# A fused transformer block: the gated linear unit and four of ten feature-major pairs computed with seven block products in place of eight

## The reference

```python
y = jax.nn.gelu(y).astype(u.dtype)                 # end of the state-space mixer
a, g = jnp.split(y @ w_glu, 2, axis=-1)            # gated linear unit, 1024 -> 2048
x = x + a * jax.nn.sigmoid(g)
x = x + sqrelu_mlp(rmsnorm(x, norm_ffn[i]), mlp_w1[i], mlp_w2[i])   # (relu(h w1))^2 w2
gate = jax.nn.sigmoid(rmsnorm(x, norm_ple[i]) @ ple_gate_w[i])
x = x + (p[i] @ ple_w[i]) * gate
x = rmsnorm(x, norm_final)
...
h = rms_norm(x, norm_g_2)                          # second block
proj = h @ w_in_2                                  # to attention, mLSTM and convolution columns
```

## Time and profile before

| what | value |
|---|---|
| median of 3 runs | 3498.07 us (3496.97 to 3499.93) |
| the profiled execution: its own time, its span | 3496.82 us, 3495.1 us |
| mean granted clock of TensorE | 0.978 of full |
| busy: PE, DVE, POOL, ACT | 94%, 53%, 41%, 32% |
| GLU, first half of the tokens: first matmul to the MLP's | 341.86 to 521.50 us |
| FM starts, first half / second half | 1280.77 / 2599.40 us |
| second half of the tokens begins | 1664.59 us |

### The profile page before, as it was taken

The page is one execution under the profiler, slowest core; times in us unless marked ns, Lnnn a source line. Parts: engine busy times, 40 slices in busy tenths (PEclk is TensorE's granted clock), DMA queues, the critical chain, the costliest instruction groups (busy, mean ns, idle before and its releaser), DMA issues. The chain is left out here.

```text
span 3495.1 us, 43699 instructions
## 1 busy us (share of the span) xinstructions
PE 3298.3 (94%) x16369; PEld 2688.0 (77%) x16369; DVE 1841.0 (53%) x2234; ACT 1133.2 (32%) x1725; POOL 1443.9 (41%) x1008
## 2 busy tenths in 40 slices
PE   5877999999999999999999999999999999697799
PEld 5655877888888778888887888888778888376687
DVE  8785126454545766970125554545766961455421
ACT  4322124333333551112224333333542111565411
POOL 6810225566666412232325565656512241243522
PEclk8988999999999999999999999999999999899899
DMA  3344211111111213233311111111213231416543
GB/s 124 102 107 113 78 49 48 55 48 54 49 53 49 95 37 127 97 121 115 121 49 48 55 49 53 49 53 50 89 48 121 93 125 55 173 63 205 175 137 116
DMA packets 155796, 301.13 MB, mean 86 GB/s; under 512 B 16640, under 2 KB 91904, under 8 KB 154000
## 3 DMA queue, kind: packets, MB, share of 16 engines
q1 hardware_dynamic: 139504, 257.23, 23.7%
q10 hardware_dynamic: 16160, 42.08, 3.1%
HBM read 226.33 MB, written 72.94 MB: 86 GB/s over the span
## 5 line engine op out<-in xcount | busy, mean ns | idle before, releaser
L1739 PE MATMUL ps_job<-AHL,WH 128*128 128x512 f32 x4480 | 1384.4, 390 | 28.6 <-POOL WL L1298 27.0
L1298 POOL TENSOR_TENSOR WL<-WR,WH 128x1024 fp32r<-128x1024 f32 x216 | 522.7, 2420 | 1205.7 <-ACT WH L996 1204.0
L1739 PEld LDWEIGHTS ps_job<-AHL,WH 128*128 128x128 f32 x4480 | 842.5, 188 | 207.3 <-issue 19.1
L1739 PE MATMUL ps_job<-AHL,WL 128*128 128x512 f32 x2240 | 873.1, 390 | 0.0
L996 ACT CAST WH<-WR 128x1024 fp32r<-128x1024 f32 x216 | 226.9, 1051 | 1007.7 <-PE ps_job L1739 823.9
L1739 PEld LDWEIGHTS ps_job<-AHL,WL 128*128 128x128 f32 x2240 | 421.7, 188 | 88.2
L1494 DVE SCALAR_TENSOR_TENSOR ps_job<-ps_job,RB 128x1024 f32<-128x1024 f32 (+1 forms) x80 | 79.9, 1017 | 410.3 <-PE ps_job L1739 396.2
L1318 POOL TENSOR_TENSOR OPS_L<-VS,OPS_H 128x1024 fp32r<-128x1024 f32 (+2 forms) x96 | 193.6, 2030 | 55.9 <-ACT OPS_H L1122 51.3
L1411 DVE TENSOR_TENSOR VS<-ps_job,VS 128x1024 f32<-128x1024 f32 x16 | 19.6, 1225 | 363.1 <-PE ps_job L1739 363.1
L1836 PE MATMUL ps_job<-OPS_H,WH 128*128 128x512 f32 x512 | 199.4, 389 | 0.7 <-POOL WL L1298 0.7
L1836 PE MATMUL ps_job<-OPS_L,WH 128*128 128x512 f32 x512 | 199.2, 389 | 0.0
(11 more groups left out here) (428 smaller groups left out, 5684.6 us busy)
## 6 DMA issues: line engine op xcount, KB each, us to landing
WR<-in_wall SPq DMA_DIRECT2D x244, 512.0 KB, 3.5
fm_scratch<-VS ACTq DMA_DIRECT2D x32, 512.0 KB, 2.6
tm_scratch<-VS ACTq DMA_DIRECT2D x24, 512.0 KB, 2.7
s_U<-in_x_group SPq DMA_DIRECT2D x8, 1024.0 KB, 14.7
s_mt<-z_scratch SPq DMA_DIRECT2D x64, 128.0 KB, 4.8
prod_scratch<-s_Win SPq DMA_DIRECT2D x16, 512.0 KB, 2.6
X<-in_x_feat SPq DMA_DIRECT2D x2, 4096.0 KB, 14.5
m_oz<-tm_scratch SPq DMA_DIRECT2D x8, 1024.0 KB, 7.7
```

What stands on the lines that cost most here:

```text
L1298: pool.tensor_tensor(dst, raw, src.bitcast(F32), ALU.subtract).then_inc(raw_free, 1)
L1739: last = pe.matmul(out, l, r, start=(k == 0 and i == 0), stop=(k == k_tiles - 1 and i == 2))
```

## The change

Each pair of weight tiles of GLU but the first two (6 of 8) and the pairs 2 to 5 of FM (tiles 4 to 11, 4 of 10) are computed as one product of 2 by 2 blocks: two output tiles, two halves of the input features, two halves of the tokens. Seven block products of 4 x 3 = 12 matmuls of 128x512 do it, 84 a pair, where two tiles took 96.

The activation blocks need four differences, `T1` to `T4`. VectorE makes them in `YR` from the unsplit activations, once for GLU and once for FM, ScalarE casts them to `T_H` (8 casts), VectorE and GpSimd subtract for `T_L` (4 each). Each pair needs the sums S1, S2, S3, S4 of its weight blocks (GpSimd, `pair_weights`), their casts (ScalarE) and low parts (GpSimd); stored tiles are the blocks W11|W12 and, in place, S3|W22. ScalarE takes three intermediate results out of PSUM (`keep_first`, `keep_second`, `keep_fifth`), VectorE puts the seven together (`corner`, `third_sum`, `first_tile`, `second_tile`).

In FM the order is changed: `copy` tiles ahead of `conv` (`KINDS`, and `ORDER` for the weights and stores); the pairs are the `silu` and `copy` tiles. The taps of the long convolution start at tile 12. `convolve` makes its first tap with an operation of three operands in place of a tensor_scalar. The rows of `X` go out in three parts in place of two, and scratch for the norms is moved.

```diff
+ORDER = [*range(0, 8), *range(16, 20), *range(8, 16)]
+N_STD, FM_END = 2, 6
-KINDS = ["c_b"] * 2 + ["c_a"] * 2 + ["silu"] * 4 + ["conv"] * 8 + ["copy"] * 4
+KINDS = ["c_b"] * 2 + ["c_a"] * 2 + ["silu"] * 4 + ["copy"] * 4 + ["conv"] * 8
-TAPS_AT = {j: 3 for j in range(4, 8)} | {j: 2 for j in range(8, 16)} | {j: 3 for j in range(16, N_COPY)}
+TAPS_AT = {j: 2 for j in range(2 * FM_END, N_FM)} | {j: 3 for j in range(N_FM, N_COPY)}
...
@@ scalar, FM @@
+                for k in range(KD // 2):
+                    act.activation(YR[:, k], X[:, k], ACT.Copy, scale=gains[:, 3, k:k + 1]).then_inc(x_raw, 1)
                 act.preload_act_table_set("natural_log_exp_and_others")
                 last_norms()
...
+                act.wait_ge(job_done, job0 + (JOB_FM + 1))
+                whi(wf + 1, 0)
+                for c, k in ((2, 0), (4, KD // 2)):
+                    act.wait_ge(t_raw, 8 * tb + 4 + c)
+                    t_high(2 * tb + 1, range(k, k + KD // 2))
+                take(0)
+                act.wait_ge(job_done, job0 + (JOB_FM + 2))
+                whi(wf + 1, 1)
...
@@ gpsimd @@
+                def pair_weights(n, w, b, first, last_free=None):
...
+                    if not first:
+                        first_tile_low()
+                    pool.wait_ge(raw_loaded[0], 16 * w2 + 16)
+                    pool.wait_ge(raw_loaded[1], 16 * w2 + 16)
+                    pool.wait_ge(q6_done, n)
+                    pool.tensor_tensor(raw[:, 0], c[:, 0:HB], c[:, HB:], ALU.add).then_inc(wsum_done, 1)
+                    pool.wait_ge(wsum_done, 3 * n + 1)
+                    pool.tensor_tensor(c[:, 0:HB], a[:, 0:HB], c[:, 0:HB], ALU.subtract).then_inc(wsum_done, 1)
+                    pool.tensor_tensor(raw[:, 1], raw[:, 0], a[:, 0:HB], ALU.subtract).then_inc(wsum_done, 1)
+                    if first:
+                        first_tile_low()
...
+                    pool.wait_ge(q3_done, n)
...
+                    pool.tensor_tensor(raw[:, 2], a[:, HB:], raw[:, 1], ALU.subtract).then_inc(raw_free, 1)
...
+                    pool.wait_ge(wsh_done, 2 * n + 1)
+                    pool.tensor_tensor(sl[:, 0:2], raw[:, 0:2], sh[:, 0:2].bitcast(F32), ALU.subtract).then_inc(wsl_done, 1)
+                    pool.wait_ge(hi_done, w + 2)
+                    pool.tensor_tensor(WL[1][:], c[:], WH[1][:].bitcast(F32), ALU.subtract).then_inc(raw_free, 1)
+                    pool.wait_ge(wsh_done, 2 * n + 2)
+                    pool.tensor_tensor(sl[:, 2], raw[:, 2], sh[:, 2].bitcast(F32), ALU.subtract).then_inc(wsl_done, 1)
...
@@ vector, FM @@
+                dve.tensor_tensor(f11, f12, f11, ALU.subtract).then_inc(t_raw, 1)
...
+                for k in range(KD // 2):
+                    step = scaled_less(YR[:, k, half(1)], KD // 2 + k, 1, YR[:, k, half(1)])
+                step.then_inc(t_raw, 1)
+                for k in range(KD // 2):
+                    step = scaled_less(YR[:, KD // 2 + k, half(0)], KD // 2 + k, 1, YR[:, k, half(0)])
+                step.then_inc(t_raw, 1)
+                dve.wait_ge(t_raw, 4 * n + 3)
+                for k in range(KD // 2):
+                    step = scaled_less(YR[:, KD // 2 + k, half(1)], KD // 2 + k, 0, YR[:, KD // 2 + k, half(0)])
+                step.then_inc(t_raw, 1)
+                dve.wait_ge(t_raw, 4 * n + 4)
                 last_norms()
...
@@ tensor @@
+                def win_pair(n, b, slots, w, t_set, free, first):
...
+                    pe.wait_ge(wl0_done, n + 1)
+                    free(0)
+                    one(1, u, stop=False).then_inc(q1_done, 1)
+                    one(2, a).then_inc(q2_done, 1)
+                    pe.wait_ge(wsl_done, 2 * n + 1)
+                    free(1)
...
+                    one(5, v)
...
+                    pe.wait_ge(c1_kept, n + 1)
+                    one(6, u, start=False, stop=False).then_inc(q6_done, 1)
+                    pe.wait_ge(raw_free, w + 4)
+                    one(7, c).then_inc(q7_done, 1)
+                    pe.wait_ge(u2_kept, n + 1)
+                    pe.wait_ge(wsl_done, 2 * n + 2)
+                    one(3, u, start=False).then_inc(q3_done, 1)
+                    pe.wait_ge(u3_done, n + 1)
+                    one(4, c).then_inc(job_done, 2)
```

More of the change, by code:

```diff
@@ new lines, in _ @@
+                act.wait_ge(job_done, job0 + (JOB_FM + 3))
+                whi(wf + 2, 0)
+                store_rows(1)
+                act.wait_ge(st_x[0], 16 * tb + 16)
+                sums_high(n, FM)
+                store_rows(2)
+                last_sum_high(n, FM, TILE_FM + 2 * N_STD)
+                act.wait_ge(job_done, job0 + (JOB_FM + 4))
+                second_tile_high(n, wf + 2)
+                for i in range(N_STD, FM_END):
+                    n, last = N_WIN * tb + GLU_WIN + i - N_STD, i == FM_END - 1
+                    slots = [slot_of(2 * i + t) for t in range(2)]
+                    keep_first(n, FM, slots[0])
+                    act.wait_ge(q2_done, n + 1)
+                    whi(wf + i + 1, 0)
+                    if i > N_STD:
+                        finish_tile(2 * i - 2)
+                    keep_second(n, FM, slots[0])
+                    keep_fifth(n, FM, slots[1])
+                    if i > N_STD:
+                        finish_tile(2 * i - 1)
+                    if not last:
+                        sums_high(n + 1, FM)
+                        last_sum_high(n + 1, FM, TILE_FM + 2 * i + 2)
+                    act.wait_ge(job_done, job0 + (JOB_FM + 2 * i + 2))
+                    if last:
+                        whi(wf + i + 1, 1)
+                    else:
+                        second_tile_high(n + 1, wf + i + 1)
@@ L1312, in group @@
+                for s in range(2):
+                    wlo(w0 + 2 + s, s)
+                t_low(2 * tb)
+                pool.wait_ge(b12_read, tb + 1)
+                for m in range(N_STD, KD):
+                    pair_weights(N_WIN * tb + m - N_STD, w0 + 2 * m, GLU, m == N_STD)
+                for s in range(2):
+                    wlo(w0 + N_GLU + s, s)
                 def group(fg):
@@ L1472, in _ @@
+                dve.wait_ge(t_raw, 8 * tb + 4)
+                t_low(2 * tb)
+                dve.wait_ge(ld_x, 16 * tb + 16)
+                for m in range(N_STD):
+                    dve.wait_ge(job_done, job0 + 2 * m + 2)
+                    mix(m, 2 * m + 1)
                 if tb:
                     dve.wait_ge(st_g, 16 * tb)
-                for k in range(KD - 2):
-                    add_up(k, halves(RB[:]))
-                for k in range(KD - 2, KD):
-                    mix(k, k % 2)
+                for m in range(N_STD, KD):
+                    n, last, slots = N_WIN * tb + m - N_STD, m == KD - 1, (2 * m % 4, (2 * m + 1) % 4)
+                    corner(n, GLU, slots[0])
+                    for k in range(4 if last else 0):
+                        add_up(k, halves(RB[:]))
+                    third_sum(n, GLU, slots[1])
+                    for k in range(4, 6 if last else 4):
+                        add_up(k, halves(RB[:]))
+                    first_tile(n, GLU, slots[0])
+                    second_tile(n, GLU, slots[1], job0 + 2 * m + 2)
+                    dve.wait_ge(paired, 2 * n + 2)
+                    mix(m, slots[1])
@@ L1696, in _ @@
                     elif KINDS[j] == "conv":
-                        convolve(j, j - M_QK.start)
+                        convolve(j, ORDER[j] - M_QK.start)
                     elif KINDS[j] == "tm":
@@ L1812, in _ @@
                             last.then_inc(job_done, 1)
-                for j in range(2, 4):
-                    pe.wait_ge(raw_free, w0 + (j + 3))
-                    pe.wait_ge(mix_done if j % 2 else sg_done, 16 * tb + (j // 2 + 1))
-                    job(j, KD, *tile(j % 2), AH, AL)
-                with pe.Fori(1, N_GLU // 4) as b:
-                    for j in range(4):
-                        pe.wait_ge(raw_free, w0 + 4 * b + (j + 3))
-                        pe.wait_ge(mix_done if j % 2 else sg_done, 16 * tb + 2 * b + (j // 2 + 1))
-                        job(j, KD, *tile(j % 2), AH, AL)
+                for n in (1, 0):
+                    for j in range(2, 4):
+                        if n == 1:
+                            pe.wait_ge(raw_free, w0 + (j + 3))
+                            pe.wait_ge(mix_done if j % 2 else sg_done, 16 * tb + (j // 2 + 1))
+                        last = product(ps4[j][:, n], KD, lambda k: three(*tile(j % 2), AH, AL, k, half(n)))
+                        if n == 0:
+                            last.then_inc(job_done, 1)
+                    if n == 1:
+                        last.then_inc(b12_read, 1)
@@ L1823, in group @@
+                for m in range(N_STD, KD):
+                    win_pair(N_WIN * tb + m - N_STD, GLU, (2 * m % 4, (2 * m + 1) % 4), w0 + 2 * m, 2 * tb,
+                             lambda i, m=m: pe.wait_ge(mix_done if i else sg_done, 16 * tb + m + 1), m == N_STD)
```

351 lines of the change are left out of this document (273 added, 78 removed).

## The result

The changed kernel takes 3506.56 us (median of 10 runs, nine of which lie between 3502.91 and 3511.29), the kernel before 3496.31 us (10 runs, 3494.03 to 3499.93): ratio 1.003, 95% interval 1.002 to 1.004. It is slower by some 10 us, where 3479 was forecast.

What follows compares the result with a forecast made beforehand. TensorE, busy 94% of the span, was taken to bound the kernel. Per half -27.2 - 0.9 + 1.3 + 9.3 + 5.7 + 1.3 = -10.5, both -21.0, with the clock -18.7: 3479 us, range 3466 to 3492.

Steps and rivals of the forecast that it cites:

- Fewer matmuls: Pairs of GLU and FM: about 240 matmuls fewer, 27.2 us less per half.
- a pair in steady state: nothing: Later pairs: GpSimd's and VectorE's work fits in a pair's 19.0 us, 4.4 us to spare, so no cost.
- rival A: TensorE waits in every pair for GpSimd's low parts of S1 and S2; 3505 at 5.7 us of lateness; chance 0.11.
- the end of GLU: One more VectorE operation from PSUM between GLU's last matmul and the mix the MLP waits for: 1.3 us more per half.
- the clock term ahead of the MLP: Idle stretch before the MLP grows to about 4 us; one fall to half clock in two halves: 2.3 us, once.
- FM, norms: Start of FM: VectorE's differences stand ahead of the norms and delay tile 2, 9.3 us more per half.
- Rival B: Norm chain at FM's start is hidden, as if VectorE's differences filled idle time: 3446; chance 0.07.
- Order of tiles, taps, first tap of `convolve`, three stores: nothing: FM and token-major part: moved taps go where VectorE waits for nobody, eight jobs cover them; no cost.
- FM, first pair: GpSimd's 16.0 us chain (T low parts, sums, first tile's low part) makes TensorE wait: 5.7 us more per half.
- VectorE and GpSimd against each other: Ahead of FM's first pair: contention lengthens GpSimd's chain by 0 to 4.4 us; 1.3 us per half taken.
- rival C: GpSimd and VectorE block each other all along FM's chain, 4.4 us per half: 3485, or 3490 with GLU's third pair; chance 0.17.
- it adds nothing: Half clock after the 11 us idle ahead of FM's tile 2 loses 2.3 us, used up in the first pair's wait.

Runs made afterwards that it cites:

- experiment 4: Changed kernel with FM put back to ordinary tiles, old order and taps, only the new first tap of `convolve` kept; GLU's pairs stay: 3465.82 us, ratio 0.9913.
- experiment 10: Changed kernel with norms ahead of differences, ScalarE's copies behind tile 2's weight cast, three FM pairs at tiles 6 to 11, later taps: 3464.68 us, ratio 0.9898.
- Experiment 5: As experiment 4 (no pairs in FM), but with the changed kernel's order of tiles and table of taps: 3481.64 us.
- Experiments 1: Changed kernel with one tap in place of two behind each convolution tile, the rest behind token-major tiles: 3495.12 us, ratio 0.9998.
- 8: Changed kernel with norms ahead of differences, first pair's sums before GpSimd's T low parts, three FM pairs, two copied tiles last, fewer taps: 3493.51 us, ratio 0.9990.
- 9: Changed kernel with two of GpSimd's four T low parts behind first FM pair's weight work, one tap in tiles 12 to 17, none in 18, 19: 3477.76 us.
- Experiment 3: Changed kernel with six of FM's eight final scaled rows of x replaced by one-column copies on VectorE: 3497.61 us (one run).

## Why the prediction was wrong, by its own steps

**Right.** *Fewer matmuls* (240) and *a pair in steady state: nothing*: behind each first pair no pair waits for its weights, so rival A did not happen. *GLU*: forecast -15.9 a half, measured -18.1 and -16.6, and experiment 4 gives it alone: -32 us in all. Part of that agreement is luck: the end of GLU, forecast 1.3 us longer, has 1.6 us less idle time, and against it the third pair of the second half, which had 1.9 us to spare in the forecast, waits 1.43. Nor did the clock term ahead of the MLP, 2.3 us once, come: behind the 1.06 us the granted clock is 1.00. *FM, norms*: 9.3 forecast, 8.9 measured, in both halves, and experiment 10 takes it away whole. Rival B is excluded.

**The step that failed: "Order of tiles, taps, first tap of `convolve`, three stores: nothing".** It named as cover that VectorE waits for nobody in the token-major part and has eight jobs to work off the taps. That is the cover behind the place. In front of it, the copied tiles, ahead of three of which VectorE had 3.9 us of idle time, were the cover, and the new order took them away. A convolution tile with two taps fills VectorE's 10.88 us with nothing to spare (from tile 13 to tile 18 it starts one every 10.97 us, 1436.83 to 1491.66), and tiles 18 and 19, beside GpSimd's weights for the token-major part, take 2.3 and 5.8 us more than TensorE's pace. The forecast also took the new first tap for no dearer than the old; in tiles 18 and 19, beside GpSimd, it took 3.3 us. Experiment 5 prices order and taps by themselves at 15.8 us, over half of the 27.6 us between forecast and result. Experiments 1, 8 and 9 shrink the wait from 7.5 to 3.4, 0 and 1.2 us by fewer taps or by copied tiles last.

**Mis-sized: "FM, first pair" with "VectorE and GpSimd against each other", 7.0 a half.** The mechanism was rival C's; it measured 11.4. GpSimd's chain, 16.0 us by undisturbed prices, took 21.4 (from 1314.22 to 1335.65), and C's own bound of 4.4 us was too low, because its price per 1024 (0.67) was a mean over six operations of 2.39 to 3.40 us, not all of which met VectorE. Experiment 3 takes VectorE's rows away and gets 3.0 us back on the four lower parts alone. Sum of both halves: 8.8 us. The Trainium skill ("SBUF — State Buffer", section "Who interferes with whom") has issue order decide who blocks, the other waiting for the whole instruction, and counts copies among the instructions that can take the shared ports: by the three-column copy at 2.32 us in place of 0.16, the trace agrees.

**Wrong: "it adds nothing" of TensorE's clock.** For the wait ahead of tile 2 that held. It overlooked the clock behind the pair's own wait, 3.0 us in the first half and 2.2 in the second; with that of the token-major wait it is 4.7 and 5.2. The sum: 15.8 for the order with its clock, 8.8 for the pair, 5.2 for the clock behind it make 29.8; GLU gave 2.9 more than forecast, the norms cost 0.8 less, and the 2.3 of clock ahead of the MLP did not come, which leaves 23.8 of the 27.6 us between 3506.6 and 3479. With the changed kernel's own figures for the order, two waits of 7.5 and 4.7 of clock, it would be 27.7, but that execution was 4.3 us longer than the median; so some 4 us stay unassigned.

What stays open: how much of the token-major wait is VectorE held up and how much lack of slack can't be split further, since each matters only with the other; how much of it the new first tap adds; and whether the four pairs with all setup hidden would give the 22 us they remove, since no kernel here hides all of it.
